# Six expert pairs' down products moved ahead of the gate tables, and what the stages hand over kept in SBUF

## The reference

```python
h = rms_norm(x, g_mix); z = h @ w_in          # pool | q | k | v | two gates
x = x + (sigmoid(gate_pool) * y_pool + sigmoid(gate_attn) * y_attn) @ w_out
x = x + peer_layer(rms_norm(x, g_ffn), ...)   # below
return rms_norm(x, g_final)

def peer_layer(h, w_q, keys_1, keys_2, expert_down, expert_up):   # 8 heads, 128 keys, top 16
    q = (ht @ w_q).reshape(T, 8, 256)
    s1, s2 = q[..., :128] against keys_1, q[..., 128:] against keys_2
    v1, i1 = top_k(s1, 16); v2, i2 = top_k(s2, 16)
    vals, ci = top_k(all sums v1 + v2, 16)                # the choice: 16 of 128^2 experts
    e_idx = i1[ci // 16] * 128 + i2[ci % 16]; gates = softmax(vals)
    act = gelu(h . expert_down[e_idx])                    # down product
    return sum over 8 heads x 16 choices of gates * act * expert_up[e_idx]
```

## Time and profile before

| | |
|---|---|
| median of three runs | 3077.05 us |
| profiled execution | 3087.25 us, span 3085.4 us, mean clock 0.956 |
| PE, PEld | busy 2822.1 us (91%), 2468.5 us (80%) |
| DVE, ACT, POOL | busy 2334.5 us (76%), 930.0 us (30%), 2134.7 us (69%) |
| DMA | 716.48 MB, mean 232 GB/s |

### The profile page before, as it was taken

How to read it: one execution, slowest core, us unless ns; L and a number is a source line. 1 busy time by engine, 2 the same in 40 slices (tenths; PEclk the granted TensorE clock), 3 DMA queues, 4 the chain that set the end, 5 groups by cost and what they waited for, 6 DMA issues and landing times.

```text
span 3085.4 us, 40038 instructions
## 1 busy us (share of the span) xinstructions
PE 2822.1 (91%) x15235; PEld 2468.5 (80%) x15235; DVE 2334.5 (76%) x4356; ACT 930.0 (30%) x1230; POOL 2134.7 (69%) x1553
## 2 busy tenths in 40 slices
PE   7999889998890697799999999999999999999996
PEld 6688777687770686799989998899899989999995
DVE  2322397345399696588899988888888888989898
ACT  4232433232420696322222222222222222222221
POOL 4334576257475696687778887887787877878774
PEclk9899999899995898999999999999999999999998
DMA  4123421022410488988999998898889988998986
GB/s 144 35 69 96 164 69 62 28 78 79 143 42 0 129 231 234 351 320 323 331 329 329 321 332 309 316 329 326 311 323 330 326 298 330 328 331 320 327 323 221
DMA packets 268048, 716.48 MB, mean 232 GB/s; under 512 B 20496, under 2 KB 106256, under 8 KB 267728
## 3 DMA queue, kind: packets, MB, share of 16 engines
q0 software_dynamic: 111152, 404.54, 35.3%
q1 hardware_dynamic: 156704, 309.38, 30.2%
HBM read 657.47 MB, written 56.36 MB: 231 GB/s over the span
## 4 chain that ended last, share of the span: by engine, by line
PE 49%; DVE 4%; DMA 3%; POOL 2%; issue 1%; ACT 1%; DVEq 0%; SPq 0%; ACTq 0%
PE abank L1381 8%; PE abank L1383 8%; PE abank L1382 8%; PE ybank L1397 8%; PE ybank L1398 8%; PE ybank L1399 8%; DVE acc L1529 2%; DMA up<-in_up,e_idx 1%; DMA up<-in_down,e_idx 1%; POOL up L1331 1%; POOL tdown_lo L1336 1%; DVE up L1517 1%; DVE y L1576 1%; DMA e_h<-all_h 0%; DVE w_lo L1569 0%
## 5 line engine op out<-in xcount | busy, mean ns | idle before, releaser
L1381 PE MATMUL abank<-h2T_hi,tdown_hi 128*128 128x320 f32 x2048 | 634.4, 310 | 38.1 <-DVE h2T_lo L1580 30.8
L1383 PE MATMUL abank<-h2T_hi,tdown_lo 128*128 128x320 f32 x2048 | 634.3, 310 | 0.0
L1382 PE MATMUL abank<-h2T_lo,tdown_hi 128*128 128x320 f32 x2048 | 634.1, 310 | 0.0
L1529 DVE SCALAR_TENSOR_TENSOR acc<-up,e_act,acc 128x1024 f32<-128x1024 f32 x381 | 489.4, 1285 | 84.5 <-DMA up<-in_up,e_idx 67.9
L1517 DVE CUSTOM_DVE_ANT_0 up<-up,acc 128x1024 f32<-128x1024 f32 x384 | 458.4, 1215 | 115.4 <-DMA up<-in_down,e_idx 106.3
L728 POOL TENSOR_TENSOR m_wlo<-m_raw,m_whi 128x1024 fp32r<-128x1024 f32 x116 | 280.8, 2428 | 381.7 <-ACT m_whi L554 379.3
L1397 PE MATMUL ybank<-tup_hi,w_hi 128*128 128x512 f32 x1280 | 505.0, 395 | 20.4 <-DVE y L1576 18.3
L1398 PE MATMUL ybank<-tup_lo,w_hi 128*128 128x512 f32 x1280 | 504.4, 394 | 0.0
L1399 PE MATMUL ybank<-tup_hi,w_lo 128*128 128x512 f32 x1280 | 501.2, 392 | 0.0
L1331 POOL DMA_INDIRECT up<-in_up,e_idx x384 | 401.7, 1046 | 103.3 <-issue 89.2
L1331 POOL DMA_INDIRECT up<-in_down,e_idx x384 | 404.6, 1054 | 98.0 <-issue 83.6
(11 more groups left out here) (220 smaller groups left out, 4620.6 us busy)
## 6 DMA issues: line engine op xcount, KB each, us to landing
tdown<-in_downT SPq DMA_DIRECT2D x128, 512.0 KB, 6.1
tup<-in_up SPq DMA_DIRECT2D x128, 512.0 KB, 6.4
m_raw<-in_tiles SPq DMA_DIRECT2D x116, 512.0 KB, 3.3
all_table<-t_out SPq DMA_DIRECT2D x10, 4096.0 KB, 16.4
gates<-all_table SPq DMA_DIRECT2D x64, 640.0 KB, 4.8
up<-in_down,e_idx POOLq DMA_INDIRECT x384, 6.5
up<-in_up,e_idx POOLq DMA_INDIRECT x384, 6.5
m_x<-in_x SPq DMA_DIRECT2D x8, 512.0 KB, 5.6
```

The lines of the kernel that those rows point to most:

```text
L1381: nc.tensor.matmul(out, tdown_hi[:, q, at], h2T_hi[:, k, ts], start=k == 0, stop=False)
L1382: nc.tensor.matmul(out, tdown_hi[:, q, at], h2T_lo[:, k, ts], start=False, stop=False)
L1383: ins = nc.tensor.matmul(out, tdown_lo[:, q, at], h2T_hi[:, k, ts], start=False, stop=k == KD - 1)
L1529: nc.vector.scalar_tensor_tensor(out=acc[:], in0=src, scalar=act_of[:, b, k:k + 1], in1=acc[:], op0=ALU.mult, op1=ALU.add).then_inc(row_us ...
```

## The change

Pairs 4, 14, 24, 34, 44 and 54 (`PRE`) get their down products at the end of the mixer: their twelve tiles follow the weight tiles through the same ring, PE multiplies them after the last query product, ACT copies the sums to SBUF and SP writes them to DRAM (`pre`). In experts these pairs have no tdown load, no high part, no remainder and no down halves; SP loads the sums straight into `w`, and ACT applies Gelu there. For this, the activations of the dense blocks and the choices stay in SBUF from the mixer on (block 3, made in group 0, is read back from DRAM into them beside group 1's queries: ACT copies its high part after the scores of n = 7, POOL makes the remainder between the two picks of head 0). The choices aren't read back by gate_table, h2T isn't read back by experts. A down product's two halves are 256 and 384 tokens for 320 and 320. Experts' first loads are issued by gate_table's SP. The pass in which pair p+1 is one of the six gets 3 shares of the rows, all others 10. Tiles of the mixer are placed anew in SBUF.

```diff
+PRE = list(range(4, NPAIR, 10))
+SPLIT = ((0, 2), (2, ND))
+SHARE = [3 if p + 1 in PRE else 10 for p in range(NPAIR)]
 # mixer, PE
+            pe.wait_ge(lead_low, 1)
+            for i in range(NPRE):
+                n = NG * NTILE + i
+                pe.wait_ge(w_low, n + 1)
+                if i >= NBANK // 2:
+                    pe.wait_ge(pre_kept, i - NBANK // 2 + 1)
+                for half, (a, b) in enumerate(SPLIT):
...
+                        ins = term(out, whi[:, n % RING, at], wlo[:, n % RING, at], hT[:, k, a:b], hlo[:, a:b, at],
+                                   k == 0, k == KD - 1)
+                ins.then_inc(pre_done, 1)
 # mixer, ACT
+                    if not more and n == 7:
+                        act.wait_ge(lead_in, 64)
+                        nc.scalar.activation(hT[:, :, TT], x[:, 0].rearrange("p (k n) -> p k n", k=KD),
+                                             ACT.Copy).then_inc(lead_high, 1)
 # mixer, POOL
+                if g + 1 == NG:
+                    for hd in range(PH):
+                        choose(g, hd, 0)
+                        tile_low(made[0] + 1)
+                        if hd == 0:
+                            pool.wait_ge(lead_high, 1)
+                            nc.gpsimd.tensor_tensor(*(... for v in (hlo[:, TT], x[:, 0])),
+                                                    hT[:, :, TT].bitcast(F32), ALU.subtract).then_inc(lead_low, 1)
+                        choose(g, hd, 1)
+                        tile_low(made[0] + 2)
+                    tile_low(LAST)
...
-            keep_choice(NG - 1)
 # gate_table, SP
-            sp.dma_start(const[:], io["const"]).then_inc(const_in, 16)
-            for i, name in enumerate(("sel1", "sel2", "gate")):
-                sp.dma_start(rows[:, i], scr[name][DB:NBLK].rearrange("t p n -> p t n")).then_inc(rows_in, 16)
+            late["first_loads"](sp)          # tdown, tup, idx, gate, y, gfin, h2, x2
 # experts
+            def load_pre(p, q):
+                sp.wait_ge(w_low, 2 * (p - 1) + q + 1)
+                sp.dma_start(w[:, q], scr["pre"][2 * PRE.index(p) + q]).then_inc(pre_in[q], 16)
...
+                if p + 2 in PRE:
+                    for q in range(2):
+                        load_pre(p + 2, q)
...
             def expert_gelu(p, q):
-                act.wait_ge(a_ready, 2 * p + q + 1)
+                if p in PRE:
+                    act.wait_ge(pre_in[q], 16 * (PRE.index(p) + 1))
+                    nc.scalar.activation(w[:, q], w[:, q], ACT.Gelu_apprx_tanh).then_inc(gl_ready, 1)
+                    return
```

More of the change, by code:

```diff
@@ L547, in tile_high @@
             def tile_high(to):
-                while made[0] < min(to, NG * NTILE):
+                while made[0] < min(to, LAST):
                     n = made[0]
@@ L574, in turned @@
                     gain = vecs[:, (V_GFFN if n else V_GMIX) + k:(V_GFFN if n else V_GMIX) + k + 1]
[L575 to L578, removed]
+                    nc.scalar.activation(hT[:, k, 0:TT], by_tile(bank(*job)[:]), ACT.Copy, scale=gain).then_inc(hT_ready, 1)
+                    if n and g == 0:
+                        nc.scalar.activation(h32[:, k], bank(*job)[:, TG - LEAD:], ACT.Copy, scale=gain).then_inc(h32_ready, 1)
             def keep_raw(g, i, *job):
@@ L711, in _ @@
                     turned(g + 1, 0)
-            gates_exp(NG - 1)
+            for i in range(NPRE):
+                act.wait_ge(pre_done, i + 1)
+                if i >= 2:
+                    act.wait_ge(pre_out[i % 2], 16 * (i // 2))
+                for half, (a, b) in enumerate(SPLIT):
+                    ins = nc.scalar.activation(pre[:, i % 2, a * P:b * P], banks[2 * i % NBANK + half][:, 0:(b - a) * P], ACT.Copy)
+                ins.then_inc(pre_kept, 1)
+                tile_high(NG * NTILE + i + RING + 1)
+                if i == NPRE - RING - 1:
+                    gates_exp(NG - 1)
         @block.gpsimd
@@ L802, in _ @@
                         through("b", m + 1)
+                    if g and m + 1 == KD:
+                        through("out", 1)
                     if g and m >= 2:
@@ L1186, in row_at @@
     return ROWS.index((kind, b, k))
+SHARE = [3 if p + 1 in PRE else 10 for p in range(NPAIR)]
 def rows_of_pair(p):
-    return range(p * NROW // NPAIR, (p + 1) * NROW // NPAIR)
+    a, b = (sum(SHARE[:n]) * NROW // sum(SHARE) for n in (p, p + 1))
+    return range(a, b)
 def parts(rows, shares):
@@ new lines, in normal, with experts @@
+def normal(p):
+    return p - sum(n < p for n in PRE)
+def experts(nc, io, scr, kept, late):
+    h2T_hi, h2T_lo = kept["hT"], kept["hlo"]
+    up, gates, w, w_hi, w_lo = (late[n] for n in ("up", "gates", "w", "w_hi", "w_lo"))
+    tdown, tdown_hi, tdown_lo, tup, tup_hi, tup_lo = (late[n] for n in ("tdown", "tdown_hi", "tdown_lo", "tup", "tup_hi", "tup_lo"))
+    idx, act_of, gate_of, stat, x2, h2, gfin, y = (late[n] for n in ("idx", "act", "gate", "stat", "x2", "h2", "gfin", "y"))
+    idx_in, gate_in, x2_in, h2_in, gfin_in, y_in, tdown_in, tup_in = (
+        late[f"{n}_in"] for n in ("idx", "gate", "x2", "h2", "gfin", "y", "tdown", "tup"))
@@ L1461, in _ @@
             down_high_of(0, 0)
-            act.wait_ge(h2T_in, 32)
-            for k in range(KD):
-                nc.scalar.activation(h2T_hi[:, k], h2T[:, k], ACT.Copy).then_inc(h2T_halved, 1)
             down_high_of(0, 1)
```

295 lines of the change are left out of this document (177 added, 118 removed).

## The result

The changed kernel takes 3050.42 us (median of 4 runs, 3049.72 to 3055.71) against 3077.82 (4 runs, 3076.65 to 3081.30) for the kernel before on the same chip: a ratio of 0.9912, 95% interval 0.9897 to 0.9928, 27.4 us less. The forecast was 3018.5, 58.6 us less. Sign and range held; less than half of the gain came.

What follows compares the result with a forecast made beforehand. PE was taken to bound the expert stage's 62 pairs at 27.76 us each. Terms -58 + 11 + 2.4 - 15 + 1 = -58.6 us off the 3077 median gave 3018.5 us, range 2988 to 3056.

Steps and rivals of the forecast that it cites:

- Steps 1, 2, 6, 7, 8: Moved halves fill PE's mixer hole; 256/384 split costs 0; choices to tables -13.2; experts' start -15 us; last-pass row +1.
- rival of narrow matmuls: Down products: 256-column matmuls run at the 128-column rate, 0.22 us each, some 3300 us in all; chance 0.03.
- Step 4: Normal expert passes get more rows, 12.8 on average for 12: 0.2 us for each of 57 passes, +11 us.
- Both rivals of rows: Normal passes: DVE or gathers pace them at 28.5 us (3050 us, chance 0.13), or DMA is full (3100, 0.04).
- Step 3: Six short expert passes without down halves: each saves 9.6 us after 4.4 us of stalls, -58 us together.
- (a): Short pass, first up product: PE waits 2.1 us for DVE's last w_lo, plus about 0.8 for DVE's added lateness.
- (b): Inside a short pass: DVE has 15.9 us of work against PE's 13.7.
- (c): Short pass: the saved product's DMA, Gelu and gates' product make the second or third up product wait 1 to 2 us.
- Step 5: Mixer's choices: wait for ACT's copy and POOL's remainders colliding with DVE's casts make the last choice 15.6 us later.
- rival of stretched choices: Mixer's choices: POOL collides twice a head and its late picks hold DVE, +19 us, 3037 us; chance 0.12.
- what would show it: Listed trace signs of right or wrong; second hits near 877 us would mean the ACT-copy wait was misplaced.

Runs made afterwards that it cites:

- nopre: The changed kernel without the moved down products, 12 rows in every pass, the rest of the change kept; 3072.32 us, ratio 0.9978.
- gather: The changed kernel, with POOL issuing all gathers of a short pass before it waits for any high part; 3027.19 us, ratio 0.9829.
- warm: The changed kernel with 12 products that nothing reads ahead of the fifth up product of each short pass; 3045.11 us, ratio 0.9885.
- warm2: As warm, with 8 more such products ahead of each short pass's first up product; 3045.83 us, ratio 0.9882.
- nolow: The changed kernel, with POOL making no remainders for the twelve moved tiles, all waits kept; 3042.09 us, ratio 0.9880.
- again: The kernel before, unchanged, profiled a second time; 3082.09 us.
- tuned: The changed kernel with short-pass gathers first, DVE's last rows before short passes behind w_lo, and block 3's remainder after head 1's second pick; 3013.16 us, ratio 0.9772.

## Why the forecast was half right

**Steps 1, 2, 6, 7, 8 held.** The twelve halves filled the hole. They ended at 1017.4, 2.6 us ahead of the last hits where I had 15, and still cost nothing, as PE then waited 17.2 us for the last pick. 256 columns take 0.120 us (0.119 forecast), which ends the rival of narrow matmuls; a pair is 0.09 us longer, 5.6 us in all, where I had 0 (two thirds of it are the split). The turn came 0.8 us behind the last pick, the second pass at -16.5 for -15, the tail at +1.4 for +1.

**Step 4 was too dear, and that hid a miss.** Its +11 for rows is nothing by the trace: 27.85 us with 12 rows and with 13. The experts lost 9.6 us anyway, to the longer pair and single stalls. Both rivals of rows are out: POOL, DVE and the DMA engines (328 GB/s) didn't pace a normal pass.

**Step 3, the largest error: -58 forecast, -43 by count of stops, -38.5 against nopre** (another pass of the profiled execution had a stall of 4.8 us). (a) was 9.7 us for 17.4: better than forecast. (b) and (c) together were 21.3 for 9. Over a short pass and the one ahead the trace has 44.6 to 49.7 us, and 60.2 where the one ahead is pass 42, for 44 to 47. I had asked when Gelu and the gates' product would be ready, and had added up DVE's work as if its rows were there. But POOL issues gathers in a fixed order with the remainders, and a remainder waits for ACT. ACT comes to tup only behind its high part of w, which waits for DVE's product with the gates (in one pass of the six it was PE that had yet to let go of tup), and to tdown only behind the new Gelu, which waits for the saved product. In the short passes these waits were still there (8.22 and 2.55 us in the fourth), so the gathers behind them came late. In the earlier trace rows POOL waits for ACT 64 times, and I read that as room for more gathers; it was also the place where a gather could be held. gather shows it: with POOL's waits for tup_hi at 48.4 us for 69.1 but no gather behind them, 18.8 of the 21.3 us are gone. The third part, 10.2 us of products at 0.50 clock, wasn't in my sum at all: each stop was priced at its length. The price was there to be read in the trace of before: behind a stop of 6.33 us in a normal pass eleven products follow each other 0.43 us apart. warm and warm2 show its cause.

```profile
2482.06 0.79 PE L1397 MATMUL ybank<-tup_hi,w_hi 128*128 128x512 f32 x1 [6.33 <-DVE y L1576]
2482.65 0.63 PE L1398 MATMUL ybank<-tup_lo,w_hi 128*128 128x512 f32 x1
2483.08 0.63 PE L1399 MATMUL ybank<-tup_hi,w_lo 128*128 128x512 f32 x1
```

The Trainium skill (TensorE: Matmul & The Clock Gate, "HAM oscillation — how this bites in real kernels") describes products that wait for data again and again and fall back to half rate each time, at a cost of its own. The trace agrees in part: 0.43 us for 0.229 behind a stop of 3.13 us, but full rate behind one of 3.0 us.

**Step 5: +15.6 forecast, +24.5 measured; the mechanism held, the sizes didn't.** DVE's wait ended at 881.4, 1 us sooner than the 882.5 of the sum. But from there to the hits I had 2.3 us and it was 6.0, for two operations met POOL's remainders; and the later heads paid 3.7 us each, not 2.4, because besides the one block in TENSOR_SCALAR or CAST the additions of the candidates stretch (L1002 1.26 us; 0.38 in nolow, median). What they met is POOL's second pick and not a remainder: in the changed kernel L1002 runs beside an operation of 1.44 us, in the last four heads of nolow beside one of 0.57. I also had POOL full in these heads, and it idled 3.3 us in each. nopre puts 8.8 us on the seam (3.6 forecast) and 15.7 on the moved tiles (12). Of "what would show it", hits at 887 against 884.8 forecast and 877 before said so at once. That is about half the way to the rival of stretched choices, which had +19 on this step.

The Trainium skill (SBUF — State Buffer, "Who interferes with whom") also says that a DVE instruction with two SBUF inputs contends with a GpSimd instruction that reads SBUF; I had used only its sentence on copies and casts. L1002 agrees, with 1.26 us beside the 1.44 us operation of POOL's pick and 0.18 us in nolow with POOL idle.

**The base.** Taking the sum off the median was right: the excess of the first profiled execution was chance, as again shows. Its 5 to 10 us explain why the spans of the two first profiles differ by 37.5 us and the medians by 27.4. They don't explain the forecast's miss.

What stays open: why a stop of about 1.3 us at the fifth product is left in tuned, and which of the single stalls of 4 us in normal passes are chance; neither was tried.

## What to carry to other kernels

When a pass gets shorter, go through every engine's queue in it, not its sum of work: what is queued behind a wait that doesn't shrink with the pass comes late, and a gather or load should stand ahead of such a wait. Price a stop of PE at its length and at the slow products that can stand behind it. When work is put beside an engine that shares its SBUF access with another, count each operation of the other that can be hit, by the rows where it already was, and look at all that the first engine does there, not at the new work alone.

## What the runs showed of the hardware

- PE came back at half clock (0.50) from a stop of 3.13 us and kept it for 11 products of 512 columns (0.43 us for 0.229, 0.2 us lost in each). In gather this was seen behind a stop of 2.0 us; behind the stops of up to 1.3 us in tuned it wasn't. A stop of 3.0 us in the changed kernel was followed by none at 0.43, one of 2.8 us by seven, so the length of a stop alone doesn't tell. Twelve products that nothing reads, put into the stop, kept the clock at 1.00.
- DVE's SCALAR_TENSOR_TENSOR on 128x64 took 2.29 us beside a POOL operation, 0.22 elsewhere; the addition with two SBUF inputs (128x32) 1.26 beside one of 1.44 us, 0.38 beside one of 0.57 and 0.18 with POOL idle.
- fp32r products from start to start: 256 columns 0.120 us, 320 0.147, 384 0.174, 512 0.227 to 0.228.
